# Seven products of halves instead of eight in the input projection of a hybrid layer

## The chip, the cores and the metric

The kernel runs on one core of one Trainium2 chip. The metric is the device time of the core in microseconds, as the median of several executions. The engines are named as in the profile: PE is TensorE, DVE is VectorE, ACT is ScalarE, POOL is GpSimd, SP is SyncE, which here only starts transfers. `PEld` is PE's weight load.

## The reference

All is fp32. One layer: x (512 tokens of 2048) behind 16 meta tokens, a norm, one large projection, two branches, a gated merge, an output projection and a last norm.

```python
xn = rmsnorm(h, norm_w)
proj = xn @ w_in
u_pool, z_pool, q, k, v, z_dn, b, a, gate_pool, gate_dn = jnp.split(proj, splits, axis=-1)
y_pool = (causal_multiscale_pool(u_pool, pool_mix, pool_scale) * jax.nn.silu(z_pool))
y_dn = gated_deltanet_branch(q, k, v, z_dn, b, a, conv_w, A_log, dt_bias, dn_norm_w)
merged = jax.nn.sigmoid(gate_pool) * (y_pool @ w_pool_out) + jax.nn.sigmoid(gate_dn) * (y_dn @ w_dn_out)
return h + merged @ w_o
...
qkv = causal_depthwise_conv_silu(jnp.concatenate([q, k, v], axis=-1), conv_w)
...
tmat = lax.linalg.triangular_solve(eye + lmat, eye, left_side=True, lower=True)
```

`w_in` has 2048 rows and 14368 columns: 1024 each for u and z of the pooling branch, 2048 each for q, k, v and z of the delta branch (16 heads of 128), 32 for b and a, 4096 for the two gates. The delta rule works on chunks of 128 tokens and inverts one triangular 128x128 matrix (`tmat`) for each chunk and head.

## The kernel before, in words

Tokens lie along the free axis: a block of the projection is `w_in[:, 256 columns].T @ xn.T`. An fp32 product is made of three products of a rounded kind (fp32r): with w = wh + wl and x = xh + xl they are wh·xh, wh·xl and wl·xh. ACT writes the high part `wh` as a copy (`split_hi`, L868), DVE subtracts it for the low part `wl` (`split_lo`, L1208).

The projection has 56 blocks of 256 columns: 8 of the pooling branch (u and zp, 4 times), 32 of the delta branch (k, q, v, z for each of 8 pairs of heads), 16 of the gates. A block is four `window`s of PE (L530): column tile c of 128, half h of K, eight tiles `kt` of 128 rows each, three terms. For u, k and v a term is two matmuls of 256 and 272 columns (512 and 16 meta tokens), for q of 256 and 260, for zp, z and the gates one of 512. So a block of u, k, v or q has 2·2·8·3·2 = 192 matmuls, one of the others 96.

```python
for w, xx, first, last in ((wh, xh, True, False), (wh, xl, False, False), (wl, xh, False, True)):
    for dst, c0, n in halves:
        mm = product(dst, w[:, slot, k, :], xx[:, kt, c0:c0 + n],
                     first and kt == 0, last and kt == KT - 1)
...
if k % 2 == 1:
    hook(k // 2)
```

The splits run one `window` ahead of PE or more; SP brings two halves of 1 MB of a block each into `raw` and reads ahead when they come free.

**The delta rule of a pair** is not a stage of its own. Each engine's program has a function `delta(d, m)`, m = 0 to 63, which it calls at a fixed place of the projection of the next pair: after every second `kt` of PE, and after each of four splits of a window on ACT and DVE. Engines execute in the order written, so such a step waits in line with the projection. The steps that matter here:

- m = F0+1 = 6: DVE scales the masked Gram matrix `mk` (L1418) and releases it (`mk_ready`).
- trip 1: `mk` goes to HBM (`gram_scratch`, L980 and L981) and comes back as 66 diagonal blocks of 16x16, one a partition (L1003). All of it is issued from ACT's queue.
- m = W0 = 14 and on: DVE inverts the 66 blocks by 14 steps of two small operations (L1437, L1440), NSTEP = 3 of them in an m, and turns the result (L1443, `w_turned`).
- trip 2: the inverses go out (`inverse_scratch`, L1008) and come back as `tm` and `st` in full rows (L1011 to L1013), also from ACT's queue.
- m = L0 = 29: PE waits for `tm_loaded` and starts to put the blocks together (32 matmuls of 32x16), DVE takes its result (L1450); m = R0 = 35 and on is the recurrence over chunks, m = O0 = 47 and on the output.

k, q and v go through a convolution of four taps on DVE (L1373, three times L1376, a tile of 128x528 each, two tiles for each of k, q and v) and a SiLU on ACT. After the projection follow the merge (`window_b`, weights `rawb`) and the output projection (`rawc`), which this change leaves as they are but for names of buffers.

## Time and profile before

| | us |
|---|---|
| device time, median of 3 runs | 1962.41 (1962.31 to 1963.6) |
| span of the profiled execution | 1960.8 |
| PE busy | 1931.4 (99%) |
| PEld busy | 1724.3 (88%) |
| DVE busy | 921.4 (47%) |
| ACT busy | 726.0 (37%) |
| POOL busy | 78.3 (4%) |

The profiled execution's span leaves out 1.6 us of the median run. Busy shares are over the whole span. A matmul's own duration in the profile overlaps its neighbours', so the pace of matmuls is read from the distance between two events of another engine that each end a known number of them. In a name such as `pj<-xh,wh` the output stands before the arrow.

### The profile page before, as it was taken

The page shows a single profiled execution, that of the slowest core. Times are in us where ns is not written, and L with a number is a line of the kernel's source. Part 1 is how long each engine was busy: PE and PEld are TensorE (multiplying, and loading weights), DVE is VectorE, ACT ScalarE, POOL GpSimd, SP SyncE. Part 2 cuts the span into 40 slices and gives each one's busy share as a digit, 9 for nine tenths or more (in the row PEclk, how much of TensorE's full clock was granted, in tenths as well). Part 3 has the DMA queues.
Part 4 walks back from the last instruction along what each step waited for, and adds up shares of the span by engine and source line. Part 5 has one row for each costly group of instructions (what it writes and reads, how often), then busy time and mean ns, then how long its engine had stood idle before and what let it go on. Part 6 is the DMA issues. An engine that isn't in the chain of part 4 may idle for free.

```text
span 1960.8 us, 35753 instructions
## 1 busy us (share of the span) xinstructions
PE 1931.4 (99%) x13729; PEld 1724.3 (88%) x13729; DVE 921.4 (47%) x2315; ACT 726.0 (37%) x2136; POOL 78.3 (4%) x105
## 2 busy tenths in 40 slices
PE   5999999999999999999999999999999999999998
PEld 5888899999999999999999988888888888888886
DVE  6333343656556466555646654322224444335332
ACT  5422223435353443535345353323234322224232
POOL 4000000000000000000000000000000000000000
PEclk8999999999999999999999999999999999999999
DMA  6133342433333242333334144333443534347302
GB/s 222 59 103 102 102 134 88 119 95 86 95 120 90 87 124 69 96 111 100 91 107 123 44 131 127 119 107 128 134 162 134 186 118 139 118 139 279 108 22 86
DMA packets 221302, 225.73 MB, mean 115 GB/s; under 512 B 33665, under 2 KB 197978, under 8 KB 220522
## 3 DMA queue, kind: packets, MB, share of 16 engines
q1 hardware_dynamic: 158898, 180.17, 28.1%
q10 hardware_dynamic: 55944, 22.63, 4.6%
q0 software_dynamic: 6336, 21.08, 3.4%
q8 instruction: 102, 1.67, 0.4%
q14 instruction: 22, 0.18, 0.0%
HBM read 199.65 MB, written 25.30 MB: 115 GB/s over the span
## 4 chain that ended last, share of the span: by engine, by line
PE 97%; ACT 1%; DVE 1%; issue 0%; POOL 0%; DMA 0%; ACTq 0%; SPq 0%; DVEq 0%
PE pj L530 82%; PE pg L530 10%; PE pt L530 3%; PE pt L679 1%; PE pg L781 0%; POOL xl L1696 0%; DVE fst L1233 0%; ACT xsquare L908 0%; DMA xt<-in_meta_tokens 0%; PE pj L574 0%; DVE xl L1239 0%; ACT wh L868 0%; DVE xt L1246 0%; ACT L1041 0%; ACT L1070 0%
## 5 line engine op out<-in xcount | busy, mean ns | idle before, releaser
L530 PE MATMUL pj<-xh,wh 128*128 128x512 f32 (+3 forms) x2688 | 735.1, 328 | 3.2 <-DVE wl L1208 3.1
L530 PE MATMUL pj<-xh,wl 128*128 128x512 f32 (+3 forms) x2688 | 712.4, 319 | 0.0
L530 PE MATMUL pj<-xl,wh 128*128 128x512 f32 (+3 forms) x2688 | 712.3, 319 | 0.0
L1208 DVE TENSOR_TENSOR wl<-raw,wh 128x256 fp32r<-128x256 f32 x896 | 344.2, 421 | 603.0 <-ACT wh L868 601.5
L530 PEld LDWEIGHTS pj<-xh,wh 128*128 128x128 f32 x2688 | 446.9, 189 | 43.2 <-DVE wl L1208 3.4
L530 PEld LDWEIGHTS pj<-xh,wl 128*128 128x128 f32 x2688 | 448.4, 188 | 35.9
L530 PEld LDWEIGHTS pj<-xl,wh 128*128 128x128 f32 x2688 | 448.8, 189 | 33.9 <-issue 1.0
L868 ACT ACTIVATE wh<-raw 128x256 fp32r<-128x256 f32 x896 | 307.0, 410 | 64.7 <-issue 45.0
L868 ACT ACTIVATE wh<-rawb 128x256 fp32r<-128x256 f32 (+1 forms) x224 | 85.0, 437 | 217.0 <-PE pj L530 189.8
L530 PE MATMUL pj<-yl,wh 128*128 128x512 f32 x384 | 149.5, 389 | 0.0
L530 PE MATMUL pj<-yh,wl 128*128 128x512 f32 x384 | 149.5, 389 | 0.0
L530 PE MATMUL pj<-yh,wh 128*128 128x512 f32 x384 | 149.4, 389 | 0.0
L1559 DVE TENSOR_TENSOR wl<-rawb,wh 128x256 fp32r<-128x256 f32 x192 | 69.5, 419 | 94.6 <-ACT wh L868 94.6
L1376 DVE SCALAR_TENSOR_TENSOR stg<-xin,convcur,stg 128x528 f32<-128x528 f32 x144 | 109.4, 760 | 0.2
L868 ACT ACTIVATE xin<-pj 128x512 f32<-128x512 f32 (+2 forms) x128 | 34.1, 336 | 154.3 <-PE pj L530 131.5
L1070 ACT ACTIVATE stg<-pj 128x512 f32<-128x512 f32 x32 | 19.1, 598 | 184.9 <-PE pj L530 184.9
L530 PEld LDWEIGHTS pj<-yl,wh 128*128 128x128 f32 x384 | 72.1, 188 | 15.1
L530 PEld LDWEIGHTS pj<-yh,wl 128*128 128x128 f32 x384 | 72.1, 188 | 15.0
L530 PEld LDWEIGHTS pj<-yh,wh 128*128 128x128 f32 x384 | 72.1, 188 | 14.8
L1026 ACT ACTIVATE oo<-pt,cur 128x128 f32<-128x128 f32 x64 | 20.0, 364 | 155.7 <-PE pt L530 155.7
L1582 DVE TENSOR_TENSOR gst<-gst,pj 128x512 f32<-128x512 f32 x32 | 20.6, 683 | 53.0 <-PE pj L530 53.0
L1735 POOL DMA_DIRECT2D branch_scratch<-zst x8 | 6.0, 745 | 905.4 <-DVE zst L1528 905.4
(243 smaller groups left out, 1784.3 us busy)
## 6 DMA issues: line engine op xcount, KB each, us to landing
raw<-in_w_in SPq DMA_DIRECT2D x112, 1024.0 KB, 6.2
rawb<-in_w_dn_out SPq DMA_DIRECT2D x16, 1024.0 KB, 6.3
rawb<-in_w_o SPq DMA_DIRECT2D x12, 1024.0 KB, 5.3
gates_scratch<-stg ACTq DMA_DIRECT2D x32, 256.0 KB, 2.1
rawb<-in_w_pool_out SPq DMA_DIRECT2D x8, 1024.0 KB, 5.7
gst<-gates_scratch POOLq DMA_DIRECT2D x32, 256.0 KB, 3.1
yraw<-branch_scratch SPq DMA_DIRECT2D x1, 5632.0 KB, 23.1
xt<-in_x SPq DMA_DIRECT2D x4, 1024.0 KB, 6.2
```

The costliest lines, as they stand in the source:

```text
L530: return pe.matmul(dst, lhs, rhs, start=start, stop=stop)
L679: mm = pe.transpose(pt[rows, i * P:(i + 1) * P], src, ident)
L868: return act.activation(dst, src, ACT.Copy)
L1026: act.activation(oo[:, at, :], pt[:, h * HD:(h + 1) * HD], ACT.Copy, scale=cur[:, EG, at:at + 1]).then_inc(o_inter, 1)
L1070: act.activation(gates_sb[c], pj[c][:, 0, :], ACT.Sigmoid).then_inc(proj_evac, 1)
L1208: tt(wl[:, j, 2 * q:2 * q + 2, :], raw[:, 2 * par + h, 2 * q:2 * q + 2, c * P:(c + 1) * P], wh[:, j, 2 * q:2 * q + 2, :].bitcast(F32), ALU ...
L1376: dve.scalar_tensor_tensor(acc, xin[:, src_tap:src_tap + T], w, acc, ALU.mult, ALU.add).then_inc(conv_step, 1)
L1559: tt(bwl[:, u, 2 * q:2 * q + 2, :], rawbs[u][:, 2 * q:2 * q + 2, c * P:(c + 1) * P], bwh[:, u, 2 * q:2 * q + 2, :].bitcast(F32), ALU.subtr ...
L1582: tt(gst[c][:, i, :], gst[c][:, i, :], pj[c][:, i, :], ALU.mult).then_inc(mg_step, 1)
L1735: pool.dma_start(y_d[bass.ds(PW + CW * d, CW), :].rearrange("(h e) t -> e h t", e=P), zst[:, :, :]).then_inc(y_stored, 16)
```

## The change

It does four things.

**Seven products.** A block is cut into halves of K (1024 rows), of columns (128) and of tokens (256, with 8 of the 16 meta tokens beside each half where there are meta tokens: 264; for q 260). The block product of 2x2x2 halves takes seven products of halves in place of eight, after Strassen and Winograd: of sums of `w` halves and sums of `x` halves. A product is 8 `kt` by 3 terms, in two chunks of 12 matmuls of 264, 260 or 256 columns. A block is 14 chunks, 168 matmuls; the first block has eight products and the last six, since each block makes the first product of the next one (`NEXT`). The sums of `x` are made once at the start (seven versions of `xh` and `xl`, on DVE and POOL). The sums of weights S1 to S4, 128x1024 elements each, are made by DVE in place in `raw` for every block. The differences of results are three operations on DVE (`c21`, `c22`, `c11`), with three snapshots of PSUM by ACT (`snap`).

**Splits.** 14 splits of 128x512 in a block on ACT and on DVE, four chunks ahead of PE (`AHEAD`), in five ring slots: split t+4 can be made once chunk t-1 is through. Before it was 16 splits of 128x256.

**The delta steps** m stand one to a chunk: 56 places for a pair; PE's at the end of a chunk. NSTEP is 2, W0 = 11, L0 = 26, R0 = 32, O0 = 44.

**Side work.** The first tap of each convolution goes from DVE to ACT, with the snapshots; the copies around L0 and the scaling of the output go from DVE to ACT; the difference `dec` from POOL to ACT. The convolved heads take a way through HBM (`head_scratch`) and are loaded by SP. All transfers of trips 1 and 2 go from ACT's queue to POOL's.

The diff, cut to its core:

```diff
+NEXT = 0
+ORDER_FIRST = (1, 2, 7, 6, 4, 5, NEXT, 3)
+ORDER = (7, 6, 4, 2, 5, NEXT, 3)
+ORDER_LAST = (7, 6, 4, 2, 5, 3)
+AHEAD = 4
+RINGS = 5
+HK = KH // 2
-        W0 = F0 + 9
-        NSTEP = 3
+        W0 = F0 + 6
+        NSTEP = 2
+        Q0 = W0 + 7
-            def window(cp, c, h, half, hook):
...
+            def block_products(b, par, kind, kind_next, hook):
+                order, base = order_of(b), base_of(b)
+                first = isinstance(b, int) and b == 0
+                for i, what in enumerate(order):
...
+                    elif what == 3:
+                        pe.wait_ge(add_done, added(b, "C22"))
+                    c0 = c0_of(kind_next if what == NEXT else kind)
+                    bank = bank_a[par] if what in (1, 6, 5, 3) else bank_a[1 - par] if what == NEXT else bank_c if what == 2 else bank_b
+                    opens, closes = what in (1, 2, 7, NEXT), what in (3, 2, 4)
+                    for h in range(2):
+                        chunk = 2 * i + h
+                        slot = ring_slot(b, chunk)
...
+                        pe.wait_ge(lo_done, base + chunk + 1)
+                        for k in range(HK):
+                            kt = HK * h + k
+                            for w, xx, one, last in ((wh, xh, True, False), (wh, xl, False, False), (wl, xh, False, True)):
+                                mm = pe.matmul(bank[:, c0:TH], w[:, slot, k, :], xx[what][:, kt, c0:TH],
+                                               start=opens and one and kt == 0, stop=closes and last and kt == KH - 1,
+                                               skip_group_check=True)
+                            if k == HK - 1:
+                                mm.then_inc(pe_chunk, 1)
+                            if k % 2 == 1:
+                                hook(2 * chunk + k // 2)
-            def split_lo(cp, par, j, q):
-                c, h = j // 2, j % 2
-                dve.wait_ge(hi_done, 16 * cp + 4 * j + q + 1)
-                tt(wl[:, j, 2 * q:2 * q + 2, :], raw[:, 2 * par + h, 2 * q:2 * q + 2, c * P:(c + 1) * P],
-                   wh[:, j, 2 * q:2 * q + 2, :].bitcast(F32), ALU.subtract).then_inc(lo_done, 1)
+            def split_lo(of, at):
+                what, half = order_of(of)[at // 2], at % 2
+                slot = ring_slot(of, at)
+                dve.wait_ge(hi_done, base_of(of) + at + 1)
+                tt(wl[:, slot, :, :], raw[:, SLOT_OF[what], HK * half:HK * (half + 1), :], wh[:, slot, :, :].bitcast(F32),
+                   ALU.subtract).then_inc(lo_done, 1)
+            def s2(b):
+                dve.wait_ge(raw_loaded[RF], 16 * b + 16)
+                dve.wait_ge(sum_done, summed(b, "S3"))
+                dve.wait_ge(lo_done, base_of(b) + after(order_of(b), 7))
+                tt(raw[:, RE, :, :], raw[:, RE, :, :], raw[:, RF, :, :], ALU.add).then_inc(sum_done, 1)
...
+            def c22(b, par, kind, dst):
+                dve.wait_ge(snap_done, snapped(b, "s4"))
+                dve.wait_ge(pe_chunk, base_of(b) + after(order_of(b), 5))
+                for part, cols in placed(kind, 1, dst):
+                    ins = tt(part, snap[:, 3, cols], bank_a[par][:, cols], ALU.subtract)
+                ins.then_inc(add_done, 1)
...
-                if m == F0 + 2:
-                    wait(mk_ready, 1, 1)
-                    act.dma_start(full_rows(gram_d), slots(mk)).then_inc(mk_stored, 16)
-                    act.dma_start(blocks(gram_d, NBLK - 2, NBLK).rearrange("a j c -> j a c"), tail(mk)).then_inc(mk_stored, 16)
...
-                if m == F0 + 6:
-                    wait(mk_stored, 32, 32)
-                    act.dma_start(gblk, blocks(gram_d, 0, NBLK)).then_inc(blk_loaded, 16)
-                if m == W0 + 5:
-                    wait(w_turned, 1, 1)
-                    act.wait_ge(blk_zeroed, 32)
-                    for scratch, block_of in zip(inv_d, (wblk, wtr)):
-                        act.dma_start(blocks(scratch, 0, NBLK), block_of).then_inc(w_stored, 16)
-                if m == W0 + 10:
-                    wait(w_stored, 32, 32)
-                    act.dma_start(slots(tm), full_rows(inv_d[1])).then_inc(tm_loaded, 16)
-                    act.dma_start(slots(st), full_rows(inv_d[0])).then_inc(st_loaded, 16)
-                    act.dma_start(tail(st), blocks(inv_d[0], NBLK - 2, NBLK).rearrange("a j c -> j a c")).then_inc(st_loaded, 16)
-                if m == L0 + 3:
...
+            def block_transfers(d):
+                pool.wait_ge(mk_ready, d + 1)
+                pool.dma_start(full_rows(gram_d), slots(mk)).then_inc(mk_stored, 16)
+                pool.dma_start(blocks(gram_d, NBLK - 2, NBLK).rearrange("a j c -> j a c"), tail(mk)).then_inc(mk_stored, 16)
+                pool.wait_ge(mk_stored, 32 * d + 32)
+                pool.wait_ge(norm_sum, d + 1)
+                pool.dma_start(gblk, blocks(gram_d, 0, NBLK)).then_inc(blk_loaded, 16)
+                pool.wait_ge(w_turned, d + 1)
+                pool.wait_ge(blk_zeroed, 32)
+                for scratch, block_of in zip(inv_d, (wblk, wtr)):
+                    pool.dma_start(blocks(scratch, 0, NBLK), block_of).then_inc(w_stored, 16)
+                pool.wait_ge(w_stored, 32 * d + 32)
+                pool.wait_ge(tok_done, ALL_TOK * d + META_TOK)
+                pool.dma_start(tail(st), blocks(inv_d[0], NBLK - 2, NBLK).rearrange("a j c -> j a c")).then_inc(st_loaded, 16)
+                pool.dma_start(slots(tm), full_rows(inv_d[1])).then_inc(tm_loaded, 16)
+                pool.dma_start(slots(st), full_rows(inv_d[0])).then_inc(st_loaded, 16)
+            for d in range(PAIRS):
+                block_transfers(d)
+                if d < PAIRS - 1:
+                    row_load(d + 1)
+                head_out(d)
```

The round trips. On ACT before, in pair 0 (the rows left out are splits, evacuations and token transposes):

```order
L980 DMA gram_scratch<-mk 128x8x128 [waits mk_ready]
L981 DMA gram_scratch<-mk 16x2x16
...
L1003 DMA oo<-gram_scratch 66x16x16 [waits mk_stored]
...
L1008 DMA inverse_scratch<-oo 66x16x16 [waits blk_zeroed,w_turned]
...
L1011 DMA tm<-inverse_scratch 128x8x128 [waits w_stored]
L1012 DMA st<-inverse_scratch 128x8x128
L1013 DMA st<-inverse_scratch 16x2x16
```

On POOL now, in pair 0; before, POOL had none of these. The reuse of `st` for both block buffers shows in the names:

```order
L2204 DMA gram_scratch<-mk 128x8x128 [waits mk_ready]
L2205 DMA gram_scratch<-mk 16x2x16
L2208 DMA st<-gram_scratch 66x16x16 [waits norm_sum,mk_stored]
L2212 DMA inverse_scratch<-st 66x16x16 [waits blk_zeroed,w_turned]
L2212 DMA inverse_scratch<-st 66x16x16
L2215 DMA st<-inverse_scratch 16x2x16 [waits tok_done,w_stored]
L2216 DMA tm<-inverse_scratch 128x8x128
L2217 DMA st<-inverse_scratch 128x8x128
```

Each of ACT's seven stood between splits, and the last three were written ten delta steps behind W0; now they stand in one line on POOL, with nothing between them.

The inversion of the blocks. On DVE before, from the wait for trip 1 on (register rows are left out):

```order
L1208 TENSOR_TENSOR wl<-raw,wh 128x256 [waits hi_done]
...
L1427 TENSOR_SCALAR oo<-oo 66x256 [waits blk_loaded]
L1429 MEMSET oo 66x16 [waits w_init]
L1437 TENSOR_TENSOR oo<-oo 66x14 [waits w_init]
...
L1440 TENSOR_TENSOR oo<-oo 66x14 [waits w_prod]
L1437 TENSOR_TENSOR oo<-oo 66x26 [waits w_step]
...
L1440 TENSOR_TENSOR oo<-oo 66x2x13 [waits w_prod]
L1437 TENSOR_TENSOR oo<-oo 66x36 [waits w_step]
...
L1440 TENSOR_TENSOR oo<-oo 66x3x12 [waits w_prod]
...
L1208 TENSOR_TENSOR wl<-raw,wh 128x256 [waits hi_done]
L1437 TENSOR_TENSOR oo<-oo 66x44 [waits w_step]
```

And now, at the same place of a pair:

```order
L1539 TENSOR_TENSOR wl<-raw,wh 128x512 [waits hi_done]
...
L1892 TENSOR_SCALAR st<-st 66x256 [waits blk_loaded]
L1894 MEMSET st 66x16 [waits w_init]
L1902 TENSOR_TENSOR st<-st 66x14 [waits w_init]
...
L1905 TENSOR_TENSOR st<-st 66x14 [waits w_prod]
L1902 TENSOR_TENSOR st<-st 66x26 [waits w_step]
...
L1905 TENSOR_TENSOR st<-st 66x2x13 [waits w_prod]
...
L1539 TENSOR_TENSOR wl<-raw,wh 128x512 [waits hi_done]
...
L1553 TENSOR_TENSOR raw<-raw 128x1024 [waits lo_done,sum_done]
L1902 TENSOR_TENSOR st<-st 66x36 [waits w_step]
...
L1905 TENSOR_TENSOR st<-st 66x3x12 [waits w_prod]
...
L1539 TENSOR_TENSOR wl<-raw,wh 128x512 [waits hi_done]
```

Between two splits stood six small operations and stand four now; a split has twice the elements, and a sum of weights (L1553, 128x1024) stands in the stretch too.

Where PE takes trip 2's result. Before, in the middle of a window:

```order
L530 MATMUL pj<-xh,wl 128x256
L530 MATMUL pj<-xh,wl 128x260
...
L121 ISA [waits tm_loaded]
L530 MATMUL pg<-tm,mk 32x16 [waits qk_ready]
L530 MATMUL pg<-tm,mk 32x16 x31
L530 MATMUL pj<-xh,wh 128x256
```

Now, at the end of chunk 26 of the pair:

```order
L720 MATMUL pj<-xh,wl 128x260
L685 MATMUL pg<-tm,mk 32x16 [waits tm_loaded,qk_ready]
L685 MATMUL pg<-tm,mk 32x16 x31
L720 MATMUL pj<-xh,wh 128x260 [waits lo_done]
L720 MATMUL pj<-xl,wh 128x260
```

The wait is the same; what has moved is the distance on PE between m = 6 and this row: 23 steps of two `kt` before (12 or 6 matmuls each), 21 chunks of 12 matmuls now (6 to 26).

## Rows read from the trace of the kernel before

**Rows 1.** The page: its head and the busy time of TensorE.

```profile
span 1960.8 us, 35753 instructions
...
PE 1931.4 (99%) x13729; PEld 1724.3 (88%) x13729; DVE 921.4 (47%) x2315; ACT 726.0 (37%) x2136; POOL 78.3 (4%) x105
```

**Rows 2.** The page: the chain that ended last, by engine.

```profile
PE 97%; ACT 1%; DVE 1%; issue 0%; POOL 0%; DMA 0%; ACTq 0%; SPq 0%; DVEq 0%
```

**Rows 3.** Waits of TensorE: line, releaser: us in total, times, longest.

```profile
PE pj L530 <- DVE wl L1208: 3.1, 1, 3.1
```

**Rows 4.** Windows of a pair without and one with delta steps; columns: busy (count) each.

```profile
242.00:333.20 91.20, 91.20 (x676) 87.45 (x675) 38.23 (x91) 25.20 (x83) 5.08 (x9) 1.00 0.37 117
449.40:565.10 115.70, 115.70 (x1118) 109.93 (x1117) 67.95 (x180) 49.66 (x163) 3.93 (x5) 1.00 0.33 99
```

**Rows 5.** Timeline of ScalarE, 100 to 300 us: start, busy, line, operation, idle before.

```profile
156.35 0.74 ACT L868 ACTIVATE ub<-pj 128x12 f32<-128x12 f32 x3 [8.66 <-PE pj L530]
...
168.06 0.74 ACT L868 ACTIVATE ub<-pj 128x12 f32<-128x12 f32 x3 [8.54 <-PE pj L530]
...
178.97 0.60 ACT L948 ACTIVATE szp<-pj 128x512 f32<-128x512 f32 x1 [7.73 <-PE pj L530]
...
276.61 0.66 ACT L868 ACTIVATE xin<-pj 128x4 f32<-128x4 f32 x2 [8.03 <-PE pj L530]
...
287.81 0.67 ACT L868 ACTIVATE xin<-pj 128x4 f32<-128x4 f32 x2 [8.09 <-PE pj L530]
```

**Rows 6.** Groups of instructions by form: busy us, mean ns, idle before.

```profile
L1208 DVE TENSOR_TENSOR wl<-raw,wh 128x256 fp32r<-128x256 f32 x896 | 344.2, 421 | 603.0 <-ACT wh L868 601.5
...
L1376 DVE SCALAR_TENSOR_TENSOR stg<-xin,convcur,stg 128x528 f32<-128x528 f32 x144 | 109.4, 760 | 0.2
...
L1590 DVE TENSOR_TENSOR wl<-rawb,wh 128x512 fp32r<-128x512 f32 x32 | 21.4, 688 | 35.0 <-ACT wh L868 35.0
...
L1735 POOL DMA_DIRECT2D branch_scratch<-zst x8 | 6.0, 745 | 905.4 <-DVE zst L1528 905.4
...
L1720 POOL DMA_DIRECT2D tm<-gate_sum_scratch x8 | 4.5, 564 | 0.6
```

**Rows 7.** Timeline of VectorE in one pair, 796.5 to 880 us.

```profile
810.49 1.23 DVE L1418 TENSOR_TENSOR mk<-mk,qd 128x1024 f32<-128x1024 f32 x1
811.63 0.17 DVE L1419 TENSOR_TENSOR mk<-mk,qd 16x32 f32<-16x32 f32 x1
...
823.05 0.28 DVE L1427 TENSOR_SCALAR oo<-oo 66x256 f32<-66x256 f32 x1
...
832.24 0.39 DVE L1443 COPY oo<-oo 66x256 f32<-66x256 f32 x1
...
847.02 0.34 DVE L1450 TENSOR_SCALAR dec<-pg,cst 128x128 f32<-128x128 f32 x1
```

**Rows 8.** Timeline of ScalarE and its queue in the same pair.

```profile
796.57 2.05 ACT L959 ACTIVATE kq<-stg 128x1056 f32<-128x1056 f32 x2
...
811.84 0.37 ACTq L980 DMA_DIRECT2D gram_scratch<-mk  x1
812.24 0.60 ACTq L981 DMA_DIRECT2D gram_scratch<-mk  x1
...
832.66 0.99 ACTq L1008 DMA_DIRECT2D inverse_scratch<-oo  x2
```

**Rows 9.** DMA issues: count, KB each, median us from issue to landing.

```profile
tm<-gate_sum_scratch POOLq DMA_DIRECT2D x8, 512.0 KB, 7.2
...
tm<-inverse_scratch ACTq DMA_DIRECT2D x8, 512.0 KB, 6.8
...
inverse_scratch<-in_consts POOLq DMA_DIRECT2D x2, 532.5 KB, 9.0
...
gram_scratch<-mk ACTq DMA_DIRECT2D x8, 2.0 KB, 5.6
```

**Rows 10.** Timeline of all engines at the start, 0 to 48 us.

```profile
16.22 2.47 DVE L1233 TENSOR_TENSOR fst<-pj,vcol 128x512 f32<-128x512 f32 x4
...
35.81 0.81 PE L530 MATMUL pj<-xh,wh 128*128 128x256 f32 x2 [3.11 <-DVE wl L1208]
```

More of the change, by code:

```diff
@@ L74, with base_of, order_of, after @@
 NGATE = 2 * D // CW
-CB = 512
-NCB = D // CB
 NCP = CP_GATE0 + NGATE
+SLOT_OF = {1: 0, NEXT: 0, 2: 1, 3: 1, 4: 3, 5: 3, 6: 2, 7: 2}
+RA, RB, RE, RF = range(4)
+def base_of(b):
+    return 0 if isinstance(b, int) and b == 0 else 14 * b + 2
+ALL_CHUNKS = base_of(NCP - 1) + 2 * len(ORDER_LAST)
+def order_of(b):
+    if isinstance(b, int):
+        return ORDER_FIRST if b == 0 else ORDER_LAST if b == NCP - 1 else ORDER
+    return ORDER
+def after(order, product):
+    return 2 * order.index(product) + 2
 CI = 0
@@ L361, in build @@
         TILE_ROWS = [META] + [P] * 4
-        TILE_COL = [SEQ] + [P * i for i in range(4)]
         def slot(t, i):
@@ L422, in blocks, with c0_of, delta_step, table_step @@
             return rows[:, 0:BS * C].rearrange("a (j c) -> a j c", c=C)[:, :, 0:BS]
+        def c0_of(kind):
+            return {"u": 0, "k": 0, "v": 0, "q": 4}.get(kind, MH)
+        POOL_KINDS, PAIR_KINDS, GATE_KINDS = ("u", "zp"), ("k", "q", "v", "z"), ("gate", "gate")
+        PAIR_HOOKS = 28 * len(PAIR_KINDS)
+        def delta_step(h):
+            return h // 2 if h % 2 == 0 else None
+        def table_step(h):
+            return next((m for m in range(16) if 7 * m // 4 == h), None)
+        def snapped(b, which):
+            return 3 * b + {"s1": 1, "s4": 2, "s2": 3}[which]
+        def added(b, which):
+            return 3 * b + {"C21": 1, "C22": 2, "C11": 3}[which]
+        def summed(b, which):
+            return 4 * b + {"S3": 1, "S2": 2, "S1": 3, "S4": 4}[which]
+        def ring_slot(b, at):
+            return (at + (3 if isinstance(b, int) and b == 0 else 0)) % RINGS
+        def ring_free(b, at):
+            if isinstance(b, int) and b == 0:
+                return at - RINGS + 1
+            return base_of(b) + (at - 3 if at < 4 else -4 if at == 4 else at - RINGS + 1)
+        def split_targets(b, t):
+            first, last = isinstance(b, int) and b == 0, isinstance(b, int) and b == NCP - 1
+            n = 2 * len(order_of(b))
+            if first:
+                own = [t + AHEAD]
+            else:
+                own = [3, 4] if t == 0 else [t + AHEAD]
+            found = [(b, at) for at in own if at < n]
+            if not last and t > n - AHEAD:
+                found.append((b + 1, t - n + 3))
+            return found
         block = outer.enter_context(nc.Block())
@@ L1075, in _ @@
-            for k in range(4):
-                for j in range(4):
-                    window(CP_GATE0 + k, k % 2, j, lambda q, k=k, j=j: delta(PAIRS - 1, 16 * k + 4 * j + q), gate_evac(k))
+                if m == O0 + 2:
+                    wait(o_rstd, 1, 1)
+                    for h in range(2):
+                        for at in range(h * NCH, (h + 1) * NCH):
+                            ins = act.activation(oo[:, at, :], oo[:, at, :], ACT.Copy, scale=oss[:, 1, at:at + 1])
+                        ins.then_inc(o_scaled, 1)
@@ new lines, in _, with no_event, gate_block, free @@
+            pair_blocks(0, None)
+            with dve.Fori(1, PAIRS) as p:
+                pair_blocks(p, p - 1)
+            def no_event(t):
+                return None
+            def gate_block(i, par, event, hook):
+                def free(c):
+                    if isinstance(i, int) and i == 0:
+                        dve.wait_ge(head_stored[c], 16 * 4 * PAIRS)
+                    else:
+                        dve.wait_ge(gate_stored[c], 16 * i)
+                block_steps(CP_GATE0 + i, par, "gate", [stg[:, c, :] for c in range(2)], free, event, hook)
```

1224 lines of the change are left out of this document (773 added, 451 removed).

## The prediction

> **What bounds the kernel now.** First the page: PE is busy for 1931.4 of the span's 1960.8 us [rows 1], and the chain that ended last is PE for 97% [rows 2]. Then PE's waits: the only one of the projection's matmuls is 3.1 us, once, at the start [rows 3]. PE's clock is at 2.4 GHz: both windows of a pair show the granted clock 1.00 [rows 4]. So the kernel is bound by PE's pace, and PE arithmetic taken away is time won, as long as nothing comes to wait that doesn't wait today.
>
> The windows tell what has room. A pair without delta steps takes 91.2 us and one with them 115.7, so they cost PE 24.5; DVE works for 67.95 of these 115.7 us, ACT for 49.7 [rows 4]. DVE has 48 us of slack, and this change spends it.
>
> **The arithmetic removed.** The pace comes from the distance of ACT's evacuations, each of which closes one column tile. For u it is 168.06 − 156.35 = 11.71 us for 96 matmuls, 122.0 ns each at a mean of 264 columns; for q 287.81 − 276.61 = 11.20, 116.7 ns at 258; for zp 178.97 − 168.06 = 10.91 for 48 of 512, 227.3 ns [rows 5]. The 264-column product is priced as it stands. The line through 258 and 264 gives 118.5 for 260 and 114.9 for 256 columns; half of 227.3 is 113.6 and the upper bound is 122.0, and I take 114.9, nearest to the half.
>
> - u, k, v, 20 blocks: 192 × 122.0 = 23.42, then 168 × 122.0 = 20.50; −2.93 each, −58.5.
> - q, 8 blocks: 22.40, then 168 × 118.5 = 19.91; −2.49 each, −19.9.
> - zp, z, gates, 28 blocks: 21.82, then 168 × 114.9 = 19.30; −2.52 each, −70.5.
>
> The sum is −149 us; the first block's extra product is what the last one lacks. PE's delta work is the same 24.5 us a pair. A pair then is 2 × 20.50 + 19.91 + 19.30 + 24.5 = 104.2 us if PE never waits. B and C, the merge and the output projection, are unchanged.
>
> **What DVE gets.** Per pair: 56 splits of 512 elements at 0.62 us, that is four such operations in 2.47 us [rows 10], 34.6 (one alone is 0.688 [rows 6]); 16 sums of 1024 at the 1.14 us from L1418 to the next start [rows 7], 18.2; 18 taps at about 0.68, the 0.760 of the row less the overlap of 0.08 that L1418 also shows [rows 6, 7], 12.2; 12 differences of half that size, about 0.37, 4.4; delta steps 67.95 − 38.23 = 29.7 [rows 4], less some 5 for the copies and scalings gone to ACT, 24.7. That is 94 of 104.2 us, 90% where it was 59%. ACT gets the snapshots, taps and copies and loses nothing but its queue's transfers; at 14 splits for 16 and some 24 us more it has about 75 of 104 and isn't the bound. SP's transfers are the same bytes. I cost these at nothing in themselves: PE has four chunks of splits in hand, 4 × 1.46 = 5.8 us. What isn't covered is a stretch in which DVE must stand still, and then catch up at 90%.
>
> **That stretch is the inversion.** It is one chain: `mk` ready, trip 1, the W steps, trip 2, PE at L0. Before, m = 6 to L0 had 23 steps of PE's windows; the chain's ends are L1419 at 811.63 and L1450 at 847.02, 35.4 us apart [rows 7], and PE didn't wait. Now, counted from the start of chunk 6:
>
> - `mk` ready. Before it took some 3.3 us from its step on. The slot now holds a longer split (0.62 for 0.34) and S4, a sum, stands before it: +2.8, so 6.1.
> - Trip 1. The store's issue is at 812.24 − 811.84 = 0.40 behind the first one, its small part lands 5.6 us later [rows 8, 9], and the load of 66 KB back has no row of its own; W0 starts at 823.05 [rows 7], which bounds it at 5.2. I take 3. Together 9.0 to 9.1.
> - W on DVE. Before 823.05 to 832.63 = 9.6 us, with four splits (1.4) and two taps (1.1) in it, so 7.1 for itself. Now seven splits (4.3), two sums (2.3), three taps (2.0), a difference (0.4): 16.1. DVE is in order, so whatever stands between delays it.
> - Trip 2. Two stores in 0.99 us [rows 8], some 3 to land, then `tm` in 6.8 [rows 9]: 10.8.
>
> The sum is 42.1 us. PE needs 21 chunks × 1.46 = 30.7 for the same way, less q's and z's cheaper ones, 30.2, and 3.9 for the delta matmuls between (Gram products with q, three token rounds and q's two, some 28 of 128 columns at 0.14). That is 34.1. PE waits 8 us at L0, in each pair.
>
> The POOL queue makes the trips longer. An issue there takes 564 ns with one run per partition and 745 with two [rows 6], +0.18 for a run, so 1.8 us for the eight runs of `mk` or `tm`, where ACT's took 0.37 [rows 8]; transfers of 512 KB land in 7.2 there against 6.8 [rows 9]. For trip 1 that is +1.4 for the store and about +1 for the blocks, +2.4 in all; for trip 2 two stores of 66 partitions × 16 runs, +1.5, and +1.4 for `tm`: +2.9. The wait would be 13.3. The bounds are then 8 with ACT's prices and 13.3 with POOL's; how much of an issue lies beside the landing isn't shown, so I take 10.5. For seven pairs and 8 for the last, whose blocks are gates: 82 us.
>
> The Trainium skill (SBUF — State Buffer, section "SBUF: two separate sides", the box on SWDGE) says that descriptors of transfers issued from GpSimd can't be written while VectorE runs an operation that holds the shared port, and that they run undisturbed from ScalarE's or SyncE's queue. In this trace the transfers of 512 KB from POOL's queue land in 7.2 us beside a DVE that is 59% busy [rows 9]; no run here shows them at 90%.
>
> **Start and end.** The start has three more versions of x to make, and block 0 needs split weights and sums at once. From L1233's 2.47 us for four [rows 10], the sums and low parts of x on DVE are about 20 operations of 1.1 to 1.2 us, half of it beside PE. Block 0 becomes DVE's: I get its end some 5 us later than PE alone would. The last block has six products in 17 us, and DVE's splits and differences with the gates' tail some 20: +4 with the first wait of the merge.
>
> **The sum.** 1960.8 − 149 + 82 + 5 + 4 = 1903, and the median of the runs is 1.6 above the profiled span: 1904.
>
> **The rivals.**
>
> - *The chain is hidden.* If DVE gets ahead before slot 6, and the issue lies beside PE's work, the 8 us shrink to about one: 1960.8 − 149 + 8 + 9 + 1.6 = 1830. For it: PE's wait was none before at nearly the same 35.4 us. Against: the PE time to hide it in has shrunk by the very 149 us, and W alone has grown by 6.5.
> - *POOL's trips starve (slower).* The change breaks even when (149 − 9) / 8 = 17.5 us of wait a pair. That is 9.4 above the 8 of ACT's prices: both trips together would take 29 us instead of 20. The one transfer of scattered kind on POOL, `inverse_scratch<-in_consts`, took 9.0 and the small one after a large 5.6 to 7 [rows 9]; two legs of 9 and two of 6 make 30. With that, PE waits 18.5 a pair: 1968. By the skill's box above this is the likely way, if DVE's operations are of the kind that holds the port.
> - *Products of 256 columns don't run below 122 ns.* The row for 264 is 122.0, though 264/512 of 227.3 would be 117.2; if that is a floor and not a slope, 28 blocks × 168 × 7.1 ns give 33 us back: 1937. Against: q's 116.7 at a mean of 258 [rows 5]. The Trainium skill (TensorE: Matmul & The Clock Gate, section "LDWEIGHTS (loading the stationary operand)") gives a weight load as its columns over 1.2, an estimated 107 ns for 128; that floor would lie below 114.9 and cost nothing.
> - *DVE is late everywhere.* At 90% every wait of DVE for a snapshot or a hi part (601.5 us of its idle time were waits for ACT's [rows 6]) is passed on, some 7 us a pair on top: 1904 + 56 = 1960.
>
> **How the numbers follow.** My forecast, waits of 6 to 14 us a pair, has 0.55, and by itself a range of 1868 to 1933. Hidden 0.15, starved 0.10, floor 0.12, late DVE 0.08. The range of 8 in 10 reaches to the hidden case and the floor, and leaves the starved trips and half of the late DVE out: 1822 to 1956. Two runs of the kernel before differ by 0.07%, and 0.2% (4 us) is what can be told from no change. Faster by more: 0.55 + 0.15 + 0.12 + 0.04 = 0.86; the other half of late DVE is split over the same and the slower side: same 0.03, slower 0.11.
>
> **What would show it.** In the profile after: the matmuls at 122 ns for 264 columns and 115 for 256, by the distance of two snapshots. PE's waits: one at L0 for `tm` behind trip 2 of 8 to 13 us, eight times, and nothing else above 10 us in total. DVE busy 90% in a pair's window. W's first operation to its copy in 16 us. Wrong would be: waits of PE for `wl` spread over all chunks (late DVE), a wait at L0 of 17 us or more (starved), or none (hidden); and a gate block, which has no delta steps, of 20.5 us in place of 19.3 (floor).

## The result, and the profile after

The changed kernel takes 2048.92 us (median of 4 runs, 2047.54 to 2049.38), the kernel before 1962.84 beside it: a ratio of 1.0437, 95% interval 1.0422 to 1.0452. It is 86 us slower. The forecast was 1904 with a range up to 1956; it was wrong in its sign.

The page of the changed kernel, its head, the busy times and the granted clock in 40 slices (tenths), answering to [rows 1]:

```profile
span 2046.0 us, 40708 instructions
...
PE 1866.3 (91%) x15073; PEld 1745.0 (85%) x15073; DVE 1369.3 (67%) x2484; ACT 1041.4 (51%) x2420; POOL 107.9 (5%) x142
...
PEclk8899999999898999999999899999999899999999
```

PE is busy for 65 us less than before, not 149, and not busy for 179.7 us where it was 29.4. The clock has a new digit: 8 stands in six slices, before only in the first. The mean granted clock is 0.963 where it was 0.997.

PE's waits of the changed kernel (line, releaser: us in total, times, longest), answering to [rows 3]:

```profile
PE pj L720 <- DVE wl L1539: 59.3, 47, 6.4
PE pg L954 <- ACT mk L1315: 32.2, 8, 4.5
PE pg L685 <- DMA tm<-inverse_scratch: 28.4, 8, 4.2
PE pt L852 <- ACT pt L1255: 11.2, 7, 1.7
...
PE pj L720 <- DVE stg L1587: 9.6, 3, 8.4
```

The wait of which the forecast was made, for `tm` at L0, is there eight times, but holds 28.4 us, not 82. Beside it stand waits that the forecast hadn't priced: 47 for low parts of weights, 8 of some 4 us for ACT's scaling of the output (L1315), 7 for ACT's squares of q. Of the 9.6 us for `stg`, 8.4 are a single wait at the end of the projection.

Windows of the changed kernel (busy us and count by engine, granted clock, DMA share, GB/s): the pair without delta steps, a pair with them, and three short stretches around its wait at L0. They answer to [rows 4]:

```profile
255.00:337.30 82.30, 81.39 (x674) 80.80 (x673) 71.77 (x107) 45.68 (x87) 2.99 (x7) 1.00 0.59 172
598.10:729.10 131.00, 113.51 (x1115) 109.26 (x1114) 94.21 (x186) 77.06 (x195) 8.70 (x11) 0.93 0.42 121
641.00:652.00 11.00, 7.91 (x65) 7.58 (x63) 8.61 (x13) 4.97 (x12) 2.37 (x3) 1.00 0.88 233
652.20:662.40 10.20, 9.30 (x234) 8.79 (x235) 5.32 (x12) 2.03 (x4) 0.00 (x0) 0.50 0.15 41
662.60:672.00 9.40, 9.40 (x126) 8.47 (x125) 5.55 (x7) 6.82 (x17) 0.00 (x0) 1.00 0.22 58
```

A pair without delta steps went from 91.2 to 82.3 us. This pair with them takes 131.0 (the seven take 127.1 to 132.7) where it was 115.7, though PE has 11 us less to do in it. DVE's 94.2 us there are the 94 of the forecast. The wait of 4.2 us begins in the third row and ends at 653.1; the fourth row, which begins in its last microsecond, is at a granted clock of 0.50, that is 1.2 GHz of the 2.4, for 10 us; the fifth is at full clock again.

### The profile page after: what moved, and what is told of

The parts are those of the page before. It is cut to its first block and busy times, and to the rows that moved or that the text cites. A ratio compares the mean times of both kernels' runs of the same rounds, so it can differ in the third digit from the quotient of the medians.

```text
span 2046.0 us, 40708 instructions
## 1 busy us (share of the span) xinstructions
PE 1866.3 (91%) x15073; PEld 1745.0 (85%) x15073; DVE 1369.3 (67%) x2484; ACT 1041.4 (51%) x2420; POOL 107.9 (5%) x142
## 5 line engine op out<-in xcount | busy, mean ns | idle before, releaser
L720 PE MATMUL pj<-xh,wh 128*128 128x256 f32 (+2 forms) x3136 | 934.7, 298 | 79.7 <-DVE wl L1539 59.3
L720 PE MATMUL pj<-xl,wh 128*128 128x256 f32 (+2 forms) x3136 | 902.2, 288 | 0.0
L720 PE MATMUL pj<-xh,wl 128*128 128x256 f32 (+2 forms) x3136 | 900.8, 287 | 0.0
L1539 DVE TENSOR_TENSOR wl<-raw,wh 128x512 fp32r<-128x512 f32 x784 | 525.6, 687 | 324.1 <-ACT wh L1045 321.3
L720 PEld LDWEIGHTS pj<-xh,wh 128*128 128x128 f32 x3136 | 609.4, 194 | 99.7 <-DVE wl L1539 50.0
L1045 ACT ACTIVATE wh<-raw 128x512 fp32r<-128x512 f32 x784 | 473.3, 626 | 425.7 <-PE pj L720 247.9
L720 PEld LDWEIGHTS pj<-xl,wh 128*128 128x128 f32 x3136 | 610.9, 195 | 1.0 <-issue 1.0
L720 PEld LDWEIGHTS pj<-xh,wl 128*128 128x128 f32 x3136 | 609.1, 194 | 0.0
L685 PE MATMUL pj<-yh,bwh 128*128 128x512 f32 x384 | 149.8, 390 | 0.4 <-DVE yl L2043 0.4
L1553 DVE TENSOR_TENSOR raw<-raw 128x1024 f32<-128x1024 f32 x56 | 68.6, 1225 | 6.3
L1559 DVE TENSOR_TENSOR raw<-raw 128x1024 f32<-128x1024 f32 x56 | 68.4, 1222 | 2.2
L1546 DVE TENSOR_TENSOR raw<-raw 128x1024 f32<-128x1024 f32 x56 | 68.1, 1216 | 1.6 <-DMA raw<-in_w_in 1.6
L1564 DVE TENSOR_TENSOR raw<-raw 128x1024 f32<-128x1024 f32 x56 | 68.3, 1219 | 0.9
```

Source lines behind the costliest of these rows:

```text
L685: return pe.matmul(dst, lhs, rhs, start=start, stop=stop)
L720: mm = pe.matmul(bank[:, c0:TH], w[:, slot, k, :], xx[what][:, kt, c0:TH], start=opens and one and kt == 0, stop=closes and last and kt == ...
L1045: return act.activation(dst, src, ACT.Copy)
L1539: tt(wl[:, slot, :, :], raw[:, SLOT_OF[what], HK * half:HK * (half + 1), :], wh[:, slot, :, :].bitcast(F32), ALU.subtract).then_inc(lo_don ...
L1546: tt(raw[:, RE, :, :], raw[:, RE, :, :], raw[:, RA, :, :], ALU.add).then_inc(sum_done, 1)
L1553: tt(raw[:, RE, :, :], raw[:, RE, :, :], raw[:, RF, :, :], ALU.add).then_inc(sum_done, 1)
```

## The experiments

Each was run beside the kernel before on one chip; three chips were used, and the kernel before had a median of 1962.4 to 1963.3 us on each. Times are medians; waits and clocks are those of one profiled run of each kernel.

### Waits and the clock, in the kernel before

```diff
-        L0 = W0 + 15
+        L0 = W0 + 10
```

> The kernel before, with L0 and all behind it five steps earlier (L0 = W0+10), so that PE must wait for tm in each pair, some 5 us, eight times; no work is added or taken away. Waits alone: 1963 + 40 = 2003. If a wait of this length by itself brings PE's clock down for a while, another 3.4 us or more in each pair: 2030 or more, with the granted clock of the pairs at 0.95 to 0.97 where it was 1.00. If the clock of the changed kernel falls for another reason than waits, the clock stays at 1.00 here.

Measured: 2027.27 us (2020.86 to 2038.5), ratio 1.032 (1.029 to 1.0349): 3 below the "2030 or more" of the clock theory and 24 above the sum of waits. The profiled run (a span of 2036.9 us, the slowest of the four) has this wait, and around the first of its eight these windows:

```profile
PE pg L530 <- DMA tm<-inverse_scratch: 46.0, 8, 6.3
```

```profile
370.00:379.60 9.60, 7.65 (x65) 7.44 (x63) 4.65 (x14) 2.99 (x11) 0.00 (x0) 1.00 0.78 212
379.90:396.90 17.00, 12.90 (x250) 11.69 (x251) 6.12 (x16) 2.56 (x8) 0.00 (x0) 0.51 0.27 69
397.00:407.00 10.00, 10.00 (x133) 9.43 (x132) 5.59 (x13) 0.35 (x2) 0.00 (x0) 0.99 0.01 2
```

Eight waits hold 46 us, and PE's busy time went from 1931.4 to 1960.8 us with the very same instructions. The middle row shows why: behind the wait, PE runs at a granted clock of 0.51 for 17 us, in the part with the many 32x16 and 32x32 matmuls; a row later it is back at 0.99. In the kernel before, where the same matmuls follow without a wait, the clock stays at 1.00. Behind the other seven waits the lower level lasted 7 to 17 us. So waits of 5 to 6 us cost their own length and half as much again (46 us of them made the profiled span 76 us longer, the median 65), in a kernel that has nothing else of the change. This was the theory of the clock, and it held: the forecast had priced waits as lengths only.

### The delta steps' places

The first kernel moves only what follows the scaling on ACT, the second also L0:

```diff
-                    if m == O0 + 3 + h:
+                    if m == O0 + 5 + h:
...
-                    if m == O0 + 4 + h:
+                    if m == O0 + 6 + h:
```

> The changed kernel with the output transposes of PE and the step of DVE behind them two chunks later (O0+5 and O0+6 in place of O0+3 and O0+4); the scaling on ACT, for which PE waited 32.2 us in 8 waits, stays at O0+2. By the sum of waits alone: 2049 - 32 = 2017. If each wait also brings the half clock that stood beside it (6.8 us in most pairs, 3.4 us lost each), another 27 go: 1990. If DVE's load is what counts, the time comes back as waits for wl, and it stays above 2035.

Measured: 2045.87 us, ratio 1.0421 (1.0404 to 1.0438), 3 us less where 32 or 59 were expected. It stayed above 2035, as in the third case, but not for that case's reason: the waits for `wl` fell, from 59.3 to 49.4. PE's waits:

```profile
PE pg L685 <- DMA tm<-inverse_scratch: 32.1, 8, 5.4
PE pj L720 <- DVE stg L1587: 31.1, 10, 8.4
...
PE pg L954 <- ACT mk L1315: 11.5, 7, 1.6
PE pj L720 <- issue: 11.0, 5, 2.7
```

The wait at the transposes (L954) fell from 32.2 to 11.5 us, and 31.1 stand at C22 (`stg`) and 11.0 at the jumps in its place. What ACT does at this time shows why. In the changed kernel, ACT's timeline in one pair:

```profile
702.75 1.28 ACT L1310 ACT_TABLE_LOAD   x1
...
704.16 0.61 ACT L1045 ACTIVATE wh<-raw 128x512 fp32r<-128x512 f32 x1
...
705.06 1.28 ACT L1213 ACT_TABLE_LOAD   x1
...
706.90 0.39 ACT L1315 ACTIVATE mk<-mk,oss 128x128 f32<-128x128 f32 x1
...
707.20 2.14 ACT L1315 ACTIVATE mk<-mk,oss 128x128 f32<-128x128 f32 x7
709.24 1.14 ACT L1045 ACTIVATE wh<-raw 128x512 fp32r<-128x512 f32 x2
```

And DVE:

```profile
709.89 0.69 DVE L1539 TENSOR_TENSOR wl<-raw,wh 128x512 fp32r<-128x512 f32 x1 [4.28 <-ACT wh L1045]
```

Two loads of activation tables (Sqrt for the output's norm, back to SiLU for the convolution), a SiLU and eight scalings take ACT 6.5 us, from 702.75 to 709.24, with one split of a high part between them, where PE needs one every 1.4 us. From 704.77 on there is none for 4.5 us, and DVE stands still for 4.28. That is shorter than the 5.8 us of reserve; in the changed kernel PE is stopped first by the scaling itself, which stands at the end of this line. With PE's step for the scaling moved out of the way, the next thing that needs this stretch of ACT and DVE waits, which is C22.

The second kernel:

```diff
-        L0 = W0 + 15
+        L0 = W0 + 18
...
-                sp.wait_ge(pe_chunk, base_of(CP_PAIR0 + 4 * d + 3))
+                sp.wait_ge(pe_chunk, base_of(CP_PAIR0 + 4 * d + 3) + 4)
```

> As e1_tr_late, and L0 with all behind it three chunks later (L0 = W0+18); the load of kq for the next pair waits four chunks longer. Waits alone: the 28.4 us for tm go too, 1989. With the clock: PE's half-clock intervals behind L0 (3.4 to 13.7 us) go as well, and nearly all of the 70 us lost to the clock comes back, 1930 to 1945. If the trips over POOL's queue are what matters, nothing remains to be gained by them beyond the 28. If DVE's load rules, waits for wl rise from 59 us to about 100 and the time stays above 2010.

Measured: 1997.12 us, ratio 1.018 (1.0161 to 1.0199), 49 less than e1, with a mean granted clock of 0.982 in place of 0.964. Between the two profiled runs, PE's time not busy fell by 29 us and its busy time by 23.5 with the same matmuls: that part is clock. What remains:

```profile
PE pj L720 <- DVE wl L1539: 50.5, 42, 6.1
PE pj L720 <- DVE stg L1587: 23.0, 12, 8.4
PE pj L720 <- issue: 22.5, 10, 3.9
```

The time is above both sums, 1989 and 1930 to 1945: more than the 28 us of the wait came back against e1, but the waits for C22 and at the jumps kept some 45.

### The jump at the end of a pair

"Issue" in that list is a wait for nothing that the profile shows. ACT at the end of a pair of e2:

```profile
700.69 0.63 ACT L1045 ACTIVATE wh<-raw 128x512 fp32r<-128x512 f32 x1 [2.03 <-DVE raw L1553]
...
704.33 1.15 ACT L1045 ACTIVATE wh<-raw 128x512 fp32r<-128x512 f32 x2 [3.01 <-issue]
```

ACT and DVE stand still for 3 us between the last instruction of a loop's body and the first of the next round, at each of the six jumps (seven rounds); in the changed kernel it is 2.8 to 5.2 us. In the kernel before, ACT and DVE are idle for some 6 us at this place, but it is PE that ends it, and PE doesn't wait. The page counts instruction packets of queue 14: 22 before, 89 in the changed kernel. The trace has their times: in the changed kernel four of them fall into each of the six standstills, and four so close together stand nowhere else behind the start; between 465 and 1115 us there are 52 of them, over five rounds, where the kernel before has none in its five from 450 to 1029 us. So the changed loop's code is loaded again in each round, and at the jump ACT and DVE wait for it.

```diff
-            with dve.Fori(1, PAIRS) as p:
+            for p in range(1, PAIRS):
                 pair_blocks(p, p - 1)
```

and so on ACT and PE.

> The changed kernel with the loop over pairs written out on PE, ACT and DVE, the same instructions without a jump. In the changed kernel ACT and DVE stand still for 2.7 to 5.0 us after each of the six jumps at the end of a pair, which the kernel before doesn't show. If that standstill is code that must be loaded again, and it feeds PE's waits, it goes: 6 times up to 4 us and the half clock it brings, 2049 - 25 to 40 = 2009 to 2024. If DVE's and ACT's four chunks of reserve hide it, 2049 stays.

Measured: 2022.99 us, ratio 1.03 (1.0283 to 1.0318): 26 less, at the small end of what was expected. The packets of queue 14 fell to 50. The half clock was not among the gain: the mean granted clock of the profiled runs is 0.963 in both. The waits for `tm`, L954 and the squares stayed at 30.4, 31.2 and 12.0 us.

> The kernel of e2_tr_l0_late with the loop over pairs written out. There 22.5 us of PE's waits (3.9 each) stand right behind the six jumps. Code theory: they go, with the half clock beside them, 1997 - 23 - 10 = 1960 to 1970. If the waits come from DVE's load, they turn into waits for wl and the time stays above 1985.

Measured: 1957.47 us (1956.08 to 1965.41), ratio 0.9978 (0.9962 to 0.9993): 40 less than e2, a little below the range expected, and just below the kernel before. Of the 22.5 us at the loop's end, 1.1 are left.

> The kernel before with the loop over pairs written out on PE, ACT and DVE. Its trace shows no standstill at the end of a pair, so code loading at the jump should cost it nothing: 1962 to 1964. If writing the loop out helps for another reason (register work of waits), it gets faster here too, by up to 10 us, and part of e5's gain isn't the jump's.

Measured: 1965.25 us, ratio 1.0012 (1.0003 to 1.0022). Written out, the kernel before gains nothing. So it is the jump of the longer program, not the loop's register work. The profiled run (1968.88 us, one of the two slowest of ten) has something for the section on the clock: a single wait of 1.3 us of PE, released by nothing that the profile shows, stands among the 32x16 matmuls at 620.6, and the granted clock is 0.51 for the 6.9 us from 622.4:

```profile
621.89 0.28 PE L530 MATMUL pj<-xl,wh 128*128 128x260 f32 x1 [1.27 <-issue]
```

A wait of 4 us isn't needed to bring the clock down.

### ACT's scaling

```diff
-                        for at in range(h * NCH, (h + 1) * NCH):
-                            ins = act.activation(oo[:, at, :], oo[:, at, :], ACT.Copy, scale=oss[:, 1, at:at + 1])
-                        ins.then_inc(o_scaled, 1)
...
+                        own = slice(h * NCH, (h + 1) * NCH)
+                        tt(oo[:, own, :], oo[:, own, :], bc(oss[:, 1, own], HD), ALU.mult).then_inc(o_scaled, 1)
```

> As e6_l0_unroll, and the scaling of the output back on DVE as two operations of 128x512, as in the kernel before, in place of eight on ACT (2.4 us). In e2 PE waited 23 us in 12 waits for C22 while ACT worked off two table loads and the scalings. If ACT's burst is the cause: those 23 go, 1935 to 1950, faster than the kernel before. If DVE's load is, its 1.3 us more in each pair make it slower than e6.

Measured: 1945.69 us, ratio 0.9917 (0.99 to 0.9933), 12 less than e6. The wait for C22 fell from 23.9 us in 12 times to 12.7 in 6, and 8.7 of these are the single wait at the end of the projection, which has nothing to do with the scaling. Giving DVE 1.3 us more in each pair made the kernel faster: ACT's burst was the cause. (The scaling now also stands one delta step earlier, so what is shown is the burst, its length and its place together.)

### The sums

```diff
-                tt(raw[:, RE, :, :], raw[:, RE, :, :], raw[:, RA, :, :], ALU.add).then_inc(sum_done, 1)
+                tt(raw[:, RE, 0:1, 0:8], raw[:, RE, 0:1, 0:8], raw[:, RA, 0:1, 0:8], ALU.add).then_inc(sum_done, 1)
```

and so the other three.

> The changed kernel in which the four sums of weights of each block are left out but for 8 elements of one partition (their semaphores stay), so the weights of five products are not the right ones. DVE has some 18 us less to do in a pair. If DVE's load makes the waits: the 59.3 us for wl go, the start loses some 15 of its waits, the wait at L0 shrinks by the two sums in the inversion (2.3 us each pair, 18), in all 1960 without and 1920 with the clock. If the waits come from where the delta steps stand: about 2010, with the waits for tm and for ACT's scaling as they were.

Measured: 2024.39 us (2019.51 to 2039.49), 25 less. PE's waits:

```profile
PE pg L685 <- DMA tm<-inverse_scratch: 34.6, 8, 4.8
PE pj L720 <- DVE wl L1539: 33.8, 26, 5.9
```

The waits for `wl` fell from 59.3 to 33.8 us, but the one for `tm` rose from 28.4 to 34.6, since PE gets to L0 earlier, and L954 stayed at 31.9. Without this load the kernel is still 3.4% slower than before: DVE's load by itself didn't make it so.

### The queue of the trips

```diff
-                block_transfers(d)
...
+                if m == F0 + 2:
+                    wait(mk_ready, 1, 1)
+                    act.dma_start(full_rows(gram_d), slots(mk)).then_inc(mk_stored, 16)
...
+                if m == W0 + 7:
+                    wait(w_turned, 1, 1)
```

> The changed kernel with the transfers of both round trips issued from ACT's queue again (delta steps F0+2, F0+5, W0+7, W0+11) and the rest on POOL's. If POOL's queue makes the trips long (8.2 and 13.8 us in the changed kernel, my prices for ACT's queue were 9 and 10.8), the 28.4 us for tm go: 2049 - 28 - 20 = 2000. If the trips are as long on ACT's queue, or ACT has to stand still for them, 2045 to 2065.

Measured: 2010.93 us, ratio 1.0248 (1.0231 to 1.0265), 38 less. The changed kernel's transfers in one pair, on POOL's queue, then those of this kernel on ACT's:

```profile
614.00 0.90 POOL L2204 DMA_DIRECT2D gram_scratch<-mk  x1 [29.64 <-DVE mk L1884]
...
618.64 1.06 POOL L2208 DMA_DIRECT2D st<-gram_scratch  x1 [3.22 <-DMA gram_scratch<-mk]
638.80 2.03 POOL L2212 DMA_DIRECT2D inverse_scratch<-st  x2 [19.10 <-DVE st L1908]
647.31 0.53 POOL L2215 DMA_DIRECT2D st<-inverse_scratch  x1 [6.48 <-DMA inverse_scratch<-st]
647.83 0.95 POOL L2216 DMA_DIRECT2D tm<-inverse_scratch  x1
```

```profile
601.70 0.39 ACTq L1236 DMA_DIRECT2D gram_scratch<-mk  x1
...
605.12 0.30 ACTq L1241 DMA_DIRECT2D st<-gram_scratch  x1
...
625.47 0.99 ACTq L1246 DMA_DIRECT2D inverse_scratch<-st  x2
...
631.42 0.32 ACTq L1250 DMA_DIRECT2D st<-inverse_scratch  x1
631.77 0.45 ACTq L1251 DMA_DIRECT2D tm<-inverse_scratch  x1
```

Trip 2's stores took 647.31 − 638.80 = 8.5 us on POOL's queue and at most 631.42 − 625.47 = 6 on ACT's; with 4.8 and 5.5 us for `tm` (medians of issue to landing) the trip is 13.8 us against 11.8. The 2 us are half of the 4.2 that PE waited. The wait for `tm` is gone all the same, since others now come before it; in all, PE's time not busy fell by 23 us and, at a mean granted clock of 0.976 in place of 0.963, its busy time by 19. What came before it is ACT's work for PE, as ACT has to wait for DVE's results and to issue the transfers itself:

```profile
PE pg L954 <- ACT mk L1334: 32.3, 8, 4.5
PE pt L852 <- ACT pt L1274: 25.4, 8, 3.2
```

### Together

Against e7_scale_dve:

```diff
-        W0 = F0 + 6
+        W0 = F0 + 7
...
-        L0 = W0 + 18
+        L0 = W0 + 17
...
-                      Q0: [("q", i) for i in range(0, 4)], Q0 + 2: [("q", i) for i in range(4, 8)]}
+                      Q0: [("q", i) for i in range(0, 4)], Q0 + 3: [("q", i) for i in range(4, 8)]}
```

> As e7_scale_dve, with W0 one chunk later (F0+7, L0 and what follows stay where they are) and the second round of q's token transposes three chunks behind the first, not two. In e7 PE waits 1.7 us in each pair for ACT's squares of the first round (12.1 in all) and some 3 us for wl in the slots of the inversion. If these waits come from where the steps stand: the 12 go and some of the 50 us for wl, 1930 to 1936. If DVE's and ACT's load makes them, they move to other rows and it stays at 1946.

As Q0 is W0 + 7, the first round of q's transposes moves by one chunk too.

Measured: 1928.44 us (5 runs, 1926.8 to 1930.88), ratio 0.983 (0.9816 to 0.9843), a little below the range expected. The 12 us for the squares went and the waits for `wl` fell from 50.2 to 35.8, while those for `xin` (C22 of k, q and v) rose from 3.8 to 14.0. So part of the waits moved to another row, as the second case said, but the larger part came from where the steps stood. It is the fastest of those that compute the layer, 1.7% below the kernel before and 120 us below the changed one, with all arithmetic as in the changed kernel. Its page and one of its pairs:

```profile
span 1925.2 us, 38552 instructions
...
PE 1825.7 (95%) x15073; PEld 1708.1 (89%) x15073; DVE 1376.0 (71%) x2500; ACT 1018.9 (53%) x2356; POOL 107.9 (6%) x142
```

```profile
585.00:698.00 113.00, 107.23 (x1119) 103.79 (x1119) 95.00 (x187) 74.30 (x188) 8.78 (x12) 1.00 0.48 139
```

The pair takes 113 us at a granted clock of 1.00, with DVE at 95.0 us of it, 84%.

> As e9_token_rounds, with the transfers of both trips on ACT's queue (F0+2, F0+6, W0+7, W0+11). In e8 that was worth 38 us, where PE waited for tm. Here L0 stands late enough that PE waits 1 us or less for tm: if the 38 us were the trip's length alone, nothing is left to gain and the time is within 5 us of e9. If transfers from POOL's queue also slow DVE or ACT in another way, it is faster by 10 us or more.

Measured: 1946.34 us, ratio 0.9918 (0.9902 to 0.9933): 18 more than e9. I had not put this among the outcomes. PE's waits name it:

```profile
PE pt L852 <- ACT pt L1274: 17.6, 8, 2.2
...
PE pt L852 <- ACT vtok L1272: 8.6, 8, 1.7
```

L1274 are the squares of q. They stand in the same delta step as the stores of trip 2 (Q0 = W0 + 7), behind them in ACT's line:

```profile
608.07 0.38 DVE L1921 COPY st<-st 66x256 f32<-66x256 f32 x1
```

```profile
608.48 1.54 ACTq L1246 DMA_DIRECT2D inverse_scratch<-st  x2
610.06 0.26 ACT L1274 ACTIVATE pt<-pt 128x128 f32<-128x128 f32 x1 [3.89 <-issue]
```

ACT has nothing else to do from 606.2 on: it waits for the turned inverses of DVE, issues the two stores and only then squares what PE waits for. With L0 late enough and the steps at these places, POOL's queue is the better one for the trips, since nobody is queued behind them there. Whether ACT's queue would do as well with the stores behind the squares wasn't run.

> As e9_token_rounds with the four sums of weights of each block left out but for 8 elements of one partition, so that the products are of other weights. This asks what DVE's load still costs once no wait stands in the delta chain: if waits for wl are load, 50 us of them shrink to about 20 and some clock returns, 1890 to 1905. If the load is covered, within 8 us of e9.

Measured: 1892.45 us, ratio 0.9654 (0.963 to 0.9677), 36 less than e9. The waits for `wl` fell from 35.8 to 18.3 us, those for C22 (`xin` and `stg`) from 24.7 to 9.0. With no stalled chain in the way, this is what DVE's load still costs, more than the 25 us of e3.

## Why the prediction was wrong

**The sum, term by term**, on the profiled spans, 1902.3 forecast and 2046.0 measured, 143.7 apart:

- *PE's arithmetic, −149.* Right but for the pace of 256 columns (by the starts of matmuls, 264 columns took 120.6 ns where 122.0 were forecast and 260 took 119.4 for 118.5, which nearly cancel). Two snapshots of ACT that stand one gate block apart in the changed kernel:

```profile
1412.20 0.37 ACT L1045 ACTIVATE snap<-pj 128x256 f32<-128x256 f32 x1
...
1432.08 0.37 ACT L1045 ACTIVATE snap<-pj 128x256 f32<-128x256 f32 x1
```

19.88 us for 168 matmuls are 118.3 ns each. The line through 258 and 264 columns had given 114.9 and 19.30 us; the rival of a floor at 122.0 had 20.50. The 0.58 us in 28 blocks are 16 us. The line was wrong in its lower point: q's 116.7 ns at a mean of 258 columns comes from the one pair without delta steps [rows 5]; in the seven other pairs of the kernel before the same mix of matmuls starts every 118.3 ns. Why that pair is faster isn't known.
- *The clock, 0.* Missing altogether. PE's busy time should have been 1931.4 − 149 = 1782 and is 1866.3, 84 more. Less the 16 of the pace, 68 are PE at half clock; 0.997 − 0.963 of 2046 us makes 70. This is the largest error, and it isn't a size but a step that was left out: the forecast read the granted clock of 1.00 in [rows 4], priced 8 to 13 us of waiting in each pair as a length alone, and didn't ask what had kept the clock up. PE never waited in these stretches. e4 shows that the wait is enough.
- *Waits, 82 + 5 + 4 = 91.* PE's time not busy rose by 150 us, 59 more. In the pair from 598 to 729 us: 4.2 for `tm`, 4.5 for ACT's scaling, 5.3 for `wl`, 1.7 for the squares, 1.8 others, 17.5 in all where 10.5 were forecast. That is the 17.5 at which the prediction saw the change break even without the clock.

The three errors, 16 + 68 + 59, are 143 of the 143.7 us. Without the 68 of the clock the change would have been some 17 us behind the kernel before, close to a tie.

Two sums of the prediction don't come out, without effect on the forecast: the pair without waits is 2 × 20.50 + 19.91 + 19.30 + 24.5 = 104.7 us, not 104.2, and trips of 30 us make PE wait 18.1 us, not 18.5.

**The chain of the inversion** was described rightly and sized well. `mk` was stored at 614.00, W began at 622.2, was turned at 638.8, and `tm` released PE at 653.10: 8.2 us for trip 1 (9.1 and 11.5 were the bounds), 16.6 for W (16.1), 14.3 for trip 2 (10.8 and 13.7). PE waited for only 4.2 of it, as it had lost 7 us in the same pair before it got there. So the one wait for which the forecast had 82 us held 28.4, and the rest of the 150 came from places that it had priced at nothing. The starved trips of the slower rival didn't come: the transfers of 512 KB on POOL's queue landed in 3.3 to 5.7 us (medians by tile) beside a DVE that was 72% busy in the pair, less than the 7.2 of [rows 9]. For them the Trainium skill's rule (SBUF — State Buffer, section "SBUF: two separate sides") isn't borne out by a delay here; most of DVE's operations in this stretch have two sources. The scattered stores of trip 2 took 8.5 us in this pair, against at most 6 from ACT's queue in e8; 1.0 of the difference is the longer issue. In e9 one pair's took 6.3 from POOL's. What the rest is, no run shows. The price of an issue was too high: `mk`'s and `tm`'s took 0.90 and 0.95 us, not 1.8.

**ACT "isn't the bound"** is the sentence that failed next. Its 77 us of 131 say nothing of order: a table load of 1.28 us, a SiLU and eight scalings stood before one split, and another load shortly before. PE waited 4.5 us for the scaling in the profile's row:

```profile
708.22 1.12 PE L954 MATMUL pg<-cst,mk 128*128 128x128 f32 x4 [4.47 <-ACT mk L1315]
```

e1 showed that the wait only moves when what waits is moved, e7 that it goes when the burst does.

**The jump** was not in any of the prediction's parts. It could be seen only in the profile after, and cost 26 us (e5).

**Late DVE**, the rival with 0.08, was partly right: 59.3 us of waits for `wl`. But e3 and e7 rank it: taking 18 us a pair from DVE won 25, and giving it 1.3 more, with ACT's burst gone, won 12. In e9, with the stalls gone, the same load costs 36 (e11).

**The start** was forecast at +5 and is worse. DVE's first operation of pair 0 (the copy of `convcur`) begins at 255.0 us where it was 244.3, 10.7 later, although eight blocks of the pooling branch were to save 21.8 and only one extra product of 2.9 was to come: some 30 us in place of 5. Between 35.6 and 255 us PE isn't busy for 18.0 us, most of it in waits for `wl`, at a granted clock of 0.95. **The end** was forecast at +4: the one wait of 8.4 us for C22 stands there, where DVE makes two low parts of the merge's input between any two splits of the last block, and the clock is at its lower level for 10.2 us from 1591.0 on, half of it behind the wait. None of the runs changed the start or the end, and both are still in e9.

What stays open: how long a body may be before it is loaded again in each round. The trace has 316 instructions of DVE and 220 of ACT in a round of the kernel before, and 354 and 365 in the changed one; no run lies between. Open too is what the start of e9, with a granted clock of 0.89 over its first 145 us, would give back.

## What to carry to other kernels

A kernel whose TensorE never waits has its clock for nothing. A change that takes arithmetic away and leaves a wait of 4 us in each round must be charged for the wait, for half of the stretch at the lower level behind it (3 to 17 us in these runs), and for all that stands in the same line; so price the longest stall, not the mean load. Look at a side engine's order before giving it work: the question is what stands between two instructions for which the bound engine is queued, and a burst near the length of the reserve is a wait, whatever the engine's share. And a loop's body that grows may cost a standstill at its jump: look at the engines' first idle time behind the last instruction of a round.
